# Linear attention of a hybrid mixer: exponents as TensorE products with 0/1 tables, 64x64 score blocks, one norm figure per head and token

## What is computed

```python
def step(state, inp):
    qc, kc, vc, gc = inp
    b = jnp.cumsum(gc, axis=2)
    o_inter = jnp.einsum('bhtd,bhdv->bhtv', qc * jnp.exp(b), state)
    decay = jnp.exp(jnp.where(causal, b[:, :, :, None, :] - b[:, :, None, :, :], -jnp.inf))
    scores = jnp.einsum('bhtd,bhtsd,bhsd->bhts', qc, decay, kc)
    o = o_inter + jnp.einsum('bhts,bhsv->bhtv', scores, vc)
    ...
o_hg = chunked_gated_linear_attention(silu(hq), -expm1(log_f), hi, log_f)
y_hg = head_rmsnorm(o_hg, hg_norm_g) * silu(hog)
```

## Time and profile before

| | us |
|---|---|
| median of 3 runs | 2489.2 (2488.23 to 2494.74) |
| the profiled execution, its own time | 2497.97 |
| its span | 2495.2 |
| PE busy | 2122.9 (85%) |
| DVE busy | 1505.1 (60%) |
| ACT busy | 1030.4 (41%) |
| DMA | 149 GB/s mean |
| mean granted TensorE clock | 0.901 |

### The profile page before, as it was taken

How to read it: one execution, slowest core, us unless ns; L and a number is a source line. 1 busy time by engine, 2 the same in 40 slices (tenths; PEclk the granted TensorE clock), 3 DMA queues, 4 the chain that set the end, 5 groups by cost and what they waited for, 6 DMA issues and landing times. The chain is left out here.

```text
span 2495.2 us, 39180 instructions
## 1 busy us (share of the span) xinstructions
PE 2122.9 (85%) x16362; PEld 2008.9 (81%) x16362; DVE 1505.1 (60%) x2321; ACT 1030.4 (41%) x1425; POOL 0.2 (0%) x4
## 2 busy tenths in 40 slices
PE   4867778889878777798898687899979899889997
PEld 4867667889878666678898676899979876889997
DVE  3766745578757667464687656555556745455554
ACT  3623333444336333343443333444445544344443
POOL 0000000000000000000000000000000000000000
PEclk8988779989989888699899888899998988889999
DMA  4322322469853223224698542355543521435552
GB/s 169 126 85 79 117 68 85 150 230 315 301 173 127 94 85 95 84 93 134 217 313 295 181 135 93 119 182 182 185 145 120 161 67 59 135 119 179 182 183 100
DMA packets 101119, 371.88 MB, mean 149 GB/s; under 512 B 11344, under 2 KB 11600, under 8 KB 100432
## 3 DMA queue, kind: packets, MB, share of 16 engines
q1 hardware_dynamic: 99936, 363.90, 44.0%
q10 hardware_dynamic: 1008, 5.49, 0.6%
HBM read 368.30 MB, written 1.05 MB: 148 GB/s over the span
## 5 line engine op out<-in xcount | busy, mean ns | idle before, releaser
L290 DVE TENSOR_TENSOR low<-raw,high 128x1024 fp32r<-128x1024 f32 x594 | 725.7, 1223 | 541.4 <-ACT high L287 540.8
L353 PE MATMUL ps<-hh,high 128*128 128x256 f32 x3248 | 940.8, 290 | 92.7 <-PEq L583 59.4
L354 PE MATMUL ps<-hh,low 128*128 128x256 f32 x3248 | 923.7, 284 | 0.0
L355 PE MATMUL ps<-hl,high 128*128 128x256 f32 x3248 | 922.3, 284 | 0.0
L287 ACT CAST high<-raw 128x1024 fp32r<-128x1024 f32 x594 | 619.4, 1047 | 595.2 <-PE ps L355 545.0
L353 PEld LDWEIGHTS ps<-hh,high 128*128 128x128 f32 x3248 | 635.9, 196 | 114.1 <-issue 101.6
L354 PEld LDWEIGHTS ps<-hh,low 128*128 128x128 f32 x3248 | 636.1, 196 | 1.5 <-issue 1.4
L355 PEld LDWEIGHTS ps<-hl,high 128*128 128x128 f32 x3248 | 635.3, 196 | 0.0
L1606 DVE SCALAR_TENSOR_TENSOR ada_rows<-ada_rows,c_act 128x1024 f32<-128x1024 f32 x96 | 117.4, 1223 | 47.5 <-DMA ada_rows<-in_ada 47.2
L354 PE MATMUL ps<-hidden_high_half,low 128*128 128x256 f32 x512 | 143.0, 279 | 0.0
L353 PE MATMUL ps<-hidden_high_half,high 128*128 128x256 f32 x512 | 142.9, 279 | 0.0
(11 more groups left out here) (377 smaller groups left out, 2849.8 us busy)
## 6 DMA issues: line engine op xcount, KB each, us to landing
raw<-in_stream SPq DMA_DIRECT2D x594, 512.0 KB, 3.5
ada_rows<-in_ada SPq DMA_DIRECT2D x96, 512.0 KB, 5.3
bias<-in_bias ACTq DMA_DIRECT2D x1, 1536.0 KB, 6.3
xT<-in_xT ACTq DMA_DIRECT2D x1, 1024.0 KB, 4.2
hybrid_const<-in_const ACTq DMA_DIRECT2D x1, 1024.0 KB, 10.6
c_act<-in_c SPq DMA_DIRECT2D x2, 512.0 KB, 3.5
out<-xT SPq DMA_DIRECT2D x1, 1024.0 KB, 3.9
par<-in_par ACTq DMA_DIRECT2D x1, 910.0 KB, 13.7
```

The costliest lines, as they stand in the source:

```text
L290: return dve.tensor_tensor(self.low[:, slot, :], self.raw[:, slot, :], self.high[:, slot, :].bitcast(F32), ALU.subtract)
L353: pe.matmul(out, sh, mh, start=start, stop=False, **more)
L354: pe.matmul(out, sl, mh, start=False, stop=False, **more)
L355: return pe.matmul(out, sh, ml, start=False, stop=stop, **more)
```

## The change

1. The running sums, the subtractions of `exponents` and their reference points go. PE turns the gates (`g`) to token-major by transposes, ACT rounds them to a float32r high half `gh`, DVE takes the low half `gl`. PE multiplies both with a constant 0/1 table (`sum_tables`), which gives both exponents of two levels at once, feature-major, in PSUM (`gate_sums`, 4 matmuls of 256 columns a fill, 4 fills for a pair of levels with `hg` and 2 with `gla`, in two PSUM banks). ACT takes the exponential out of PSUM. Four pairs of levels stand in steps 0, 1, 3 and 5, ahead of the step's projection pair.
2. Up to level 5 only blocks of 64x64 can hold scores, so PE makes two 64x64 blocks a tile in place of 128x128. `pick` has half as many columns. The scores of level 6 and of `cross` are copied by ACT. PV has five matmuls a head in place of three: the first 64 queries of a tile need only 64 keys.
3. The sum of squares of a head and token is made once, in 8 matmuls of one column; square root and reciprocal have 8 columns. PE spreads the reciprocal over the partitions by 8 matmuls with an identity, between the two tail pairs. Gain and gate are multiplied in before. The last product, rounding and subtraction run in two halves.
4. The tables (640 KB) are a further load at the start, staged in `sq` and rounded by ACT; the masks have 448 columns fewer. Projection pairs from the seventh on use two PSUM banks (2 and 3) in place of four, since the sums use 0 and 1.

```diff
+    s_, t_ = np.arange(P)[:, None], np.arange(P)[None, :]
+    out = []
+    for lv in range(LEVELS):
+        mid = t_ // (2 << lv) * (2 << lv) + (1 << lv)
+        out.append(np.where(t_ < mid, (s_ > t_) & (s_ < mid), (s_ >= mid) & (s_ <= t_)))
+    out += [s_ > t_, out[-1], s_ <= t_]
+    return np.concatenate(out, 1).astype(np.float32)
...
-                    prod = Product(self.w, at * BLOCKS, n, KD, banks, name in ("hi", "gv", "nvsw"))
+                    prod = Product(self.w, at * BLOCKS, n, KD, banks if len(self.pairs) < 6 else mix_banks,
+                                   name in ("hi", "gv", "nvsw"))
...
-            b = W[:, 0, 0:n]
...
-            decay = [flat(sq[:, 4 * i:4 * i + tiles, :]) for i in range(2)]
+            gh, gl = (rounded[:, i * 2 * BANK:(i + 1) * 2 * BANK].rearrange("p (t n) -> p t n", t=TT) for i in range(2))
...
+            def decay(lv):
+                return decays[lv // 2 % 2][:, lv % 2, :]
...
-                    for f in range(tiles):
+
+                    def split_gates():
+                        dve.wait_ge(g_high.sem, g_high.base + 1)
                         for t in range(TT):
...
+                            ins = dve.tensor_tensor(gl[:, t, 0:wide], ps[:, t, 0:wide], gh[:, t, 0:wide].bitcast(F32),
+                                                    ALU.subtract)
+                        tell(ins, g_low)
...
-                    def exponents(lv):
-                        if lv >= 2:
-                            dve.wait_ge(to_pe.sem, to_pe.base + lv - 1)
-                        first, second = halves(b, lv)
-                        e1, e2 = halves(decay[lv % 2], lv)
-                        ref = first[:, :, (1 << lv) - 1:1 << lv].broadcast_to(list(first.shape))
-                        dve.tensor_tensor(e1, ref, first, ALU.subtract)
...
-                        dve.wait_ge(to_dve.sem, to_dve.base + lv + 1)
+                        dve.wait_ge(decays_taken.sem, decays_taken.base + fills * (lv // 2 + 1))
...
+                        for i in range(per_head):
+                            to = scores[:, i * group:(i + 1) * group, :]
+                            seen = ps[:, bank_of(step) + i, 0:group * CHUNK].rearrange("p (h t) -> p h t", h=group)
+                            if step == 0:
+                                ins = dve.tensor_tensor(to, seen, C("eye_chunk").unsqueeze(1)
+                                                        .broadcast_to([P, group, CHUNK]), ALU.mult)
+                            else:
+                                mask = C("level", (step - 1) * CHUNK, CHUNK).bitcast(U32).unsqueeze(1) \
+                                    .broadcast_to([P, group, CHUNK])
+                                ins = dve.copy_predicated(to, mask, seen)
...
+                    for step in range(LAST + 1):
+                        if step < LAST:
                             weigh(step)
-                        pick(step)
+                        if step < LEVELS:
+                            pick(step)
                         if step:
                             for p in mine[step - 1:step]:
                                 proj.vector(dve, p)
...
+                    dve.wait_ge(pv_done.sem, pv_done.base + 1)
+                    dve.wait_ge(squares.sem, squares.base + 1)
+                    for h in range(4):
+                        cols = slice(h % 2 * T, (h % 2 + 1) * T)
+                        ins = dve.scalar_tensor_tensor(W[:, 1, h * T:(h + 1) * T], ps[:, 4 + h // 2, cols],
+                                                       gain[:, h:h + 1], gate[:, h, :], ALU.mult, ALU.mult)
+                    done(ins)
                     dve.wait_ge(summed.sem, summed.base + 1)
-                    for i in range(2):
...
+                    tell(dve.tensor_scalar(cstat[:, 0, 0:8], ps[:, 6, 0:8], 1.0 / 128, EPS, ALU.mult, ALU.add), variance)
+                    dve.wait_ge(deviation.sem, deviation.base + 1)
+                    tell(dve.reciprocal(cstat[:, 1, 0:8], cstat[:, 0, 0:8]), rstd_ready)
...
-                    done(dve.reciprocal(W[:, 0, :], W[:, 0, :]))
...
-                    tell(dve.tensor_tensor(W[:, 1, :], W[:, 1, :], flat(gate[:, :, :]), ALU.mult), to_act)
...
+                    dve.wait_ge(rstd_spread.sem, rstd_spread.base + 1)
+                    for i in range(2):
+                        half = W[:, 1, i * BANK:(i + 1) * BANK]
+                        tell(dve.tensor_tensor(half, half, ps[:, 6 + i, :], ALU.mult), to_act)
+                    for i in range(2):
+                        dve.wait_ge(to_dve.sem, to_dve.base + i + 1)
+                        c = slice(2 * i, 2 * i + 2)
+                        dve.tensor_tensor(flat(yl[:, branch, c, :]), W[:, 1, i * BANK:(i + 1) * BANK],
+                                          flat(yh[:, branch, c, :]).bitcast(F32), ALU.subtract)
                     for p in tail[1:]:
                         proj.vector(dve, p)
 
...
-                    for lv in range(LEVELS + 1):
-                        act.wait_ge(to_act.sem, to_act.base + lv + 1)
-                        tell(act.activation(decay[lv % 2], decay[lv % 2], ACT.Exp), to_dve)
...
+                    act.wait_ge(g_turned.sem, g_turned.base + 1)
+                    for t in range(TT):
+                        ins = act.copy(gh[:, t, 0:wide], ps[:, t, 0:wide])
+                    tell(ins, g_high)
...
+                    def exponentials(pair):
+                        for f in range(fills):
+                            i = pair * fills + f
+                            act.wait_ge(sums_ready.sem, sums_ready.base + i + 1)
...
+                            to = decays[pair % 2].rearrange("p l (f t s) -> p f t l s", f=fills, t=TT)
+                            seen = ps[:, i % 2, :].rearrange("p (t l s) -> p t l s", t=TT, l=2)
+                            tell(act.activation(to[:, f, :, :, :], seen, ACT.Exp), decays_taken)
+
+                    exponentials(0)
+                    for step in range(LAST + 1):
+                        if step in (1, 3, 5):
+                            exponentials((step + 1) // 2)
+                        for p in mine[step:step + 1]:
+                            proj.scalar(act, p)
+                    done = InOrder(act, act_step)
+                    act.wait_ge(prob_ready.sem, prob_ready.base + LEVELS)
+                    done(act.copy(first[0:CHUNK, :, :], scores[0:CHUNK, :, :]))
...
+                        ins = act.copy(cross[:, i * w:(i + 1) * w, :],
+                                       ps[:, bank_of(LAST) + i, 0:w * P].rearrange("p (h t) -> p h t", h=w))
+                    tell(ins, late_scores)
...
-                    tell(act.copy(flat(yh[:, branch, :, :]), W[:, 1, :]), to_dve)
+                    for i in range(2):
+                        act.wait_ge(to_act.sem, to_act.base + i + 1)
+                        tell(act.copy(flat(yh[:, branch, 2 * i:2 * i + 2, :]), W[:, 1, i * BANK:(i + 1) * BANK]), to_dve)
...
+                    for t in range(TT):
+                        for f in range(tiles):
+                            ins = pe.transpose(ps[:, t, f * P:(f + 1) * P], g[:, f, t * P:(t + 1) * P], ident)
+                    tell(ins, g_turned)
...
+                    def gate_sums(pair):
+                        for f in range(fills):
+                            i = pair * fills + f
+                            if i >= 2:
+                                pe.wait_ge(decays_taken.sem, decays_taken.base + i - 1)
+                            for t in range(TT):
+                                o = ps[:, i % 2, t * T:(t + 1) * T]
+                                at = pair * T + (t * T if pair == 3 else 0)
+                                m = tables[:, at:at + T]
+                                pe.matmul(o, gh[:, t, f * P:(f + 1) * P], m, start=True, stop=False)
+                                ins = pe.matmul(o, gl[:, t, f * P:(f + 1) * P], m, start=False, stop=True)
+                            tell(ins, sums_ready)
...
+                                for j in range(P // CHUNK):
+                                    lo = j * CHUNK
+                                    ins = pe.matmul(out_[lo:lo + CHUNK, :], head(a, h, t, lo, CHUNK),
+                                                    head(c, h, t, lo, CHUNK), start=True, stop=True)
                         tell(ins, score_done)
+                        if step == 0:
+                            pe.wait_ge(g_low.sem, g_low.base + 1)
+                            gate_sums(0)
+                        if step in (1, 3, 5):
+                            gate_sums((step + 1) // 2)
                         for p in mine[step:step + 1]:
                             proj.tensor(pe, p)
...
+                        cols = slice(h * P, (h + 1) * P)
...
+                            if t:
+                                c, c0 = cross_place(h)
```

(61 more changed lines are left out.)

144 lines of the change are left out of this document (63 added, 81 removed).

## The result

The changed kernel takes 2521.45 us, median of 4 runs (2519.22 to 2525.35), beside 2491.3 for the kernel before (4 runs). The ratio is 1.0113, 95% interval 1.0092 to 1.0135: slower by 28 us by this ratio (30 by the medians), more than three times the 8.4 of the forecast, and 2521.45 lies outside its range (2483 to 2512). The profiled execution took 2525.35 for a span of 2523.6, 28.4 more than before.

A forecast was written before the change was run, and what follows sets the result against it. PE was taken to bound the closed steps, DVE's queue the open steps and the tail. Terms of +3.2 (`hg`) and +0.4 (`gla`) in two layers plus +1.2 once gave +8.4, 2497.6 us from the median; range 2483 to 2512.

The forecast's parts named there:

- Start of the block: Transposes, gate split and first sums before the first projection, which begins at about 7.5 us in `hg`: +3.5; `gla` +3.3.
- gate_sums: Later sums of gates on PE in the closed steps: +8.5 us in `hg`, +1.9 in `gla`.
- Scores: 64x64 score blocks in closed steps, 1.2 us a step for 1.75 in `hg`: -2.75; `gla` -0.9.
- serial rival: 64x64 score blocks do not overlap, 0.056 us each: 23.2 us more, 2520.8; chance 0.13.
- The evidence for the overlap: 16 instructions of 15 stationary columns, started 0.023 us apart, taken to show that different column strips work side by side.
- Open steps: From step 6 of `hg` and step 4 of `gla` to PV: 7.3 us (-3.3) and 10.1 us (-3.4).
- PV: 40 instructions for 24, some 5 us at half clock, 8.85 us in all: +3.5 in `hg`, +5.9 in `gla`.
- Sums: Sums of squares after PV, 16 x 0.112 = 1.8 us against 1.42 in `hg`: +0.4.
- First tail pair: Projection pair behind the sums: no term of its own, a pair of the tail counted at 5.7 us.
- Spread, tail gap, start of the program: Spread of the reciprocal +1.8 us; gap before the next block near 3.8 for 12.3 (`hg` -8.5); program start +1.2, once.
- clock stays full: Rival: full clock through open steps and PV, both PVs 6.7 us: -8.6, time 2489.0; chance 0.22.
- Cheap PV: Rival: 64 moving columns cost half of 128, row changes hidden: 18.8 us less, 2478.8; chance 0.12.

The follow-up runs named there:

- e5: The kernel before with only the compact norm (part 3 of the change); 2477.5 us beside 2494.57, ratio 0.9949.
- e6: e1 with part 1 undone too (exponents on DVE, no tables, four projection banks); 2463.53 us beside 2494.57, ratio 0.9881.
- e1: The changed kernel with PV as before, three full products a head; 2487.57 us beside 2496.09, ratio 0.9968.
- e3: The kernel before with only PV split into five products a head; 2527.99 us beside 2496.09.
- e11: The changed kernel with all 40 entries of PV padded with zeros to 128 rows and 128 moving columns; 2491.32 us beside 2501.92.
- e7: e1 with 128 moving columns in the sums of squares, of which one is read; 2481.99 us beside 2494.57, ratio 0.9939.
- e4: The changed kernel with 30 further unread products a block keeping PE at work ahead of PV; 2508.58 us beside 2496.09.
- e10: The changed kernel with PV's products padded with zeros to 128 rows, their 64 moving columns kept; 2503.31 us beside 2496.39.
- e8: e6 with the wide sums of e7 (exponents on DVE, PV as before); 2454.04 us beside 2494.57, ratio 0.9849.

## Why the prediction was wrong

The ratios form a chain from the kernel before to the changed one: the compact norm (e5), then the smaller score blocks (e6), then the exponents on PE (e1), then the split PV (changed kernel). In us of 2495:

| part | forecast | measured |
|---|---|---|
| 3, compact norm | -25.4 | -13 |
| 2, score blocks and their reads | -7.3 | -17 |
| 1, exponents on PE, with the start | +22.2 | +22 |
| 2, split PV | +18.8 | +36 |
| sum | +8.3 | +28 |

The forecasts are sums over the steps of both layers. The intervals of the ratios leave the measured differences 4 to 7 us either way, and the split into parts holds for this order of the chain (e3 has +32 for the split PV alone). Point by point:

- **Start of the block,** held nearly. The projection begins 8.2 after the block's start (92.59 to 100.79) for 7.5, since `gate_sums(0)` ran at half clock, and 4.5 in `gla`.
- **gate_sums,** held. 3.6 at step 1 (forecast 3.75), with the wait for ACT seen at 110.28, then 2.5 and 2.5 (2.4), 1.06 in `gla` (0.95).
- **Scores,** held. 32 entries of 64x64 start within 1.09 us (123.64 to 124.73), forecast 1.2, before 1.75. The serial rival falls, though its 2520.8 meets the measured time: the number was right by another mechanism. The rule of the Trainium skill that spoke for it, page "TensorE: Matmul & The Clock Gate", Part 3 (a weight load overlaps a running matmul only when the row group differs), isn't borne out by this row either. In the table the part gained more than forecast: from e5 to e6 the four blocks shorten by 17 ahead of PV, of which 5 are lost again from PV on (3.4 of them in `gla` of layer 0, where PV takes 4.7 for 2.9 and the tail pair 8.3 for 7.1). Some of it is the open steps' gain, which I had booked on part 1 as a whole.
- **The evidence for the overlap** was weak, and its coming true in part luck. The earlier trace rows have entries with 15 stationary columns 0.023 apart, and 15/128 of 0.213 is 0.025: that row needs no overlap. What shows it is step 7 of the changed kernel (L1143 at 147.09), where all blocks go to the same 64 columns of the array. Its entries start 0.058 apart at full clock, the 0.056 of the serial rival, and those of the step before (L1149) in pairs 0.058 apart.
- **Open steps,** held. 7.1 (146.10 to 153.23) and 9.9 (238.41 to 248.28) for 7.3 and 10.1.
- **PV,** failed. The price at half clock was nearly right: 11.5 forecast, 12.04 measured (40 x 0.213, and 16 changes at 0.2). What failed is "I expect some 5 us at half": the clock never rose. I carried over the course of the earlier trace rows, where the low stretch lasted about as long as PV, to entries of another shape. That is 3.2 a block, 13 in all. It also left the stated bounds, +6.7 in `hg` (0 to +6) and +9.1 in `gla` (3.8 to 8.6). e11 shows that with the same entries filled up the clock does rise.
- **Sums,** failed as a consequence: 3.4 for 1.8, 1.6 a block, 6.6 in all. At full clock they take the forecast time (1.95 with the drain in e1).
- **First tail pair,** a term that the sum did not have. Its price was fixed at 5.7; it took 6.9, 7.1, 8.1 and 8.4 up to the spread, 7.7 in all. Some 5.9 of it stands in e1 too, where the sums run at full clock (7.2, the same in `hg` of e5), and goes with 128 columns (e7, 5.5). The rest stands in layer 1 alone (8.1 and 8.4), and why isn't shown. Since e11 keeps the clock up behind one-column sums in `gla`, their single column is one condition of the fall and not all of it. In e5 the same term is 5.6 of the 7.4 by which the four blocks gained less than forecast (25.4 - 18.0): in the earlier trace rows I read the price of a one-column product (L2390) and not the clock behind it. The trace of before has it, though behind other small products as well. The sums of L2390 and a stretch soon after:

```profile
2038.46:2040.30 1.84, 1.84 (x19) 1.00 0.00 0
2042.00:2046.00 4.00, 3.74 (x11) 0.50 0.02 4
```

- **Spread, tail gap, start of the program,** held: 1.7 for 1.8; 3.6 and 3.5 for 3.8; 1.7 for 1.2.

The three that failed make 13 + 6.6 + 7.7 = 27, against 31.6 - 7.2 = 24.4 by which the four blocks are longer than forecast; the small terms give 3 back. So what was mis-sized is the clock in the stretch behind the open steps, from PV to the spread (153.23 to 176.76 in `hg`), and nothing else of weight. Of the rivals, "clock stays full" was wrong in the same direction: e4 shows that even a PV that starts at full clock loses it. "Cheap PV" fell: an entry of 64 columns takes the 0.21 of one of 128 at half clock (e10: 8.76 for 40).

## What to carry to other kernels

Cut a float32 product into smaller ones only where the pieces work side by side in the array, as the 64x64 scores do: pieces that each occupy it alone save nothing at 64 moving columns, pay for every change of rows, and can hold the clock low, for themselves and for the work behind them. When a change gives products another shape, price them and what follows at half clock as well as at full, since a busy PE is no evidence of a full clock. And work that another engine did hidden beside PE isn't worth moving onto PE where PE is the bound: the exponents cost 22 us there, with what the open steps paid back already counted.

## What the runs showed of the hardware

- PE can be busy for 12.04 of 12.10 us and be granted 1.2 GHz throughout (40 entries with changing rows, most of 64 columns). 13.29 of 13.30 us did so with 128 columns.
- 16 float32 entries with a single moving column were followed by a fall of the clock inside the projection behind them in e1 and e5, and not in `gla` of e11; with 128 columns (e7, e8) they took 0.1 us more and never were. One of 128 moving columns costs hardly more than one of a single column.
- A change between products over 64 and over 128 rows costs 0.2 us at half clock, and more with 128 columns: (13.31 - 8.9) / 16 = 0.28, as 40 x 0.213 and the drain make 8.9.
- 64x64 blocks that share the rows of the array but not its columns do overlap: 32 entries in 1.09 us, 0.034 each. Where they share the columns too (step 7) they start 0.058 apart, and full entries 0.11.
- Open: whether the gate goes by moved columns, by used rows or their changes, or by something that holds all of them. No run varied one of them in steps.
